# One encoder layer with PEER experts on one core: two pieces of TensorE work stand earlier, three top-k units later, and four row pairs are handled by VectorE inside the gate round

## The reference

```
proj = x @ w_in                              # 512 tokens, D = 1024
a_out = spatial_gating(...); r_out = retention(...)
h = layer_norm(ALPHA * x + concat(a_out, r_out) @ w_out)

def peer(h, w_q, sub_keys, u_tab, v_tab):    # 128*128 experts, 8 heads, 16 chosen per head
    q = (h @ w_q).reshape(b, s, 8, 2, 128)
    scores = einsum('bshpd,hpnd->bshpn', q, sub_keys)
    top_s, top_i = top_k(scores, 16)         # per half, 128 keys
    ... # 256 sums of pairs, the 16 best: expert_idx, gates = softmax
    act = gelu(einsum('td,ted->te', h, u_tab[expert_idx]))
    return einsum('te,ted->td', gates * act, v_tab[expert_idx])

x = layer_norm(ALPHA * h + peer(h))
```

## Time and profile before

| | |
|---|---|
| median of 3 runs | 1390.03 us (1389.23 to 1395.6) |
| the profiled execution | 1392.22 us, its span 1390.2 us |
| TensorE busy | 1341.3 us, 96% of the span |
| VectorE busy | 1082.9 us, 78% |
| ScalarE, GpSimd busy | 385.7 us, 697.5 us |
| granted clock, mean | 0.988 |
| TensorE starts the first act | 410.58 us |
| the gate round on TensorE | 635.82 to 706.45 us |
| DMA | 444.22 MB, mean 320 GB/s, over 410 GB/s in most slices behind the round |

### The profile page before, as it was taken

One profiled execution on the slowest core, in us unless ns is written; L12 is line 12 of the kernel. 1 busy time (PEld: TensorE's weight loads), 2 busy tenths in 40 slices (PEclk: granted clock), 3 DMA queues, 4 the chain that ended last, 5 costly groups with the idle time before them and its releaser, 6 DMA issues.

```text
span 1390.2 us, 17959 instructions
## 1 busy us (share of the span) xinstructions
PE 1341.3 (96%) x6450; PEld 947.9 (68%) x6450; DVE 1082.9 (78%) x2459; ACT 385.7 (28%) x790; POOL 697.5 (50%) x548
## 2 busy tenths in 40 slices
PE   8999998979999999999999999999999999999996
PEld 6788755568888888887754445558888885444442
DVE  4837264699999999767996779798988889666567
ACT  4213200241220102017940025656664102000000
POOL 2325111367544548751057656545754667666370
PEclk9999999989999999999999999999999999999998
DMA  7421064489999999996169999999999999999994
GB/s 250 141 79 61 2 241 130 151 295 400 381 336 382 353 367 401 413 413 273 62 237 414 414 414 413 406 366 382 381 375 375 395 413 413 414 414 414 415 414 181
DMA packets 118424, 444.22 MB, mean 320 GB/s; under 512 B 11712, under 2 KB 24512, under 8 KB 101952
## 3 DMA queue, kind: packets, MB, share of 16 engines
q0 software_dynamic: 73728, 268.47, 49.7%
q1 hardware_dynamic: 44032, 173.56, 32.2%
q10 hardware_dynamic: 576, 1.05, 0.2%
HBM read 440.94 MB, written 2.10 MB: 319 GB/s over the span
## 4 chain that ended last, share of the span: by engine, by line
PE 82%; ACT 4%; DVE 4%; DMA 3%; PEld 2%; issue 1%; ACTq 1%; DVEq 1%; PEldq 1%; POOL 0%; SPq 0%
PE ps L1469 33%; PE ps L1557 30%; PE ps L1486 7%; DMA pool_mem<-in_peer_w_q_dram 2%; PE ps L1740 2%; PEld ps L1469 2%; PE ps L1649 2%; ACT wr L700 2%; ACT wr L702 1%; PE ps L1670 1%; PE ps L1643 1%; PE ps L1541 1%; ACTq L701 1%; PE ps L1617 1%; DVE nw L886 1%
## 5 line engine op out<-in xcount | busy, mean ns | idle before, releaser
L636 POOL DMA_INDIRECT big<-in_peer_u_dram,idx x256 | 330.7, 1292 | 353.7 <-DVE dots L1248 270.1
L650 POOL DMA_INDIRECT big<-in_peer_v_dram,idx x256 | 305.9, 1195 | 164.4 <-DVE y L1273 105.9
L1273 DVE SCALAR_TENSOR_TENSOR y<-big,wgt,y 128x1024 f32<-128x1024 f32 x256 | 328.1, 1281 | 71.8 <-DMA big<-in_peer_v_dram,idx 68.3
L1248 DVE CUSTOM_DVE_ANT_0 big<-big,xh 128x1024 f32<-128x1024 f32 x256 | 310.9, 1216 | 42.6 <-DMA big<-in_peer_u_dram,idx 42.2
L1557 PE MATMUL ps<-big,pool_mem 128*128 128x512 f32 x496 | 217.4, 593 | 0.0
L1469 PE MATMUL ps<-xT,big 128*128 128x256 f32 x960 | 211.1, 380 | 0.0
L1469 PEld LDWEIGHTS ps<-xT,big 128*128 128x128 f32 x960 | 181.7, 190 | 24.3
L1557 PEld LDWEIGHTS ps<-big,pool_mem 128*128 128x128 f32 x496 | 93.7, 190 | 114.8 <-issue 114.8
L1557 PE MATMUL ps<-y,pool_mem 128*128 128x512 f32 x256 | 113.6, 594 | 0.0
L1469 PE MATMUL ps<-xT,pool_mem 128*128 128x256 f32 (+1 forms) x512 | 102.5, 360 | 5.0 <-ACTq L792 2.4
L1557 PE MATMUL ps<-xT,pool_mem 128*128 128x512 f32 x240 | 106.4, 594 | 0.0
(11 more groups left out here) (295 smaller groups left out, 1537.8 us busy)
## 6 DMA issues: line engine op xcount, KB each, us to landing
big<-u_pairs_dram SPq DMA_DIRECT2D x32, 1024.0 KB, 8.2
big<-v_pairs_dram SPq DMA_DIRECT2D x32, 1024.0 KB, 8.0
y<-u_pairs_dram SPq DMA_DIRECT2D x16, 1024.0 KB, 8.2
xT<-u_pairs_dram SPq DMA_DIRECT2D x16, 1024.0 KB, 7.9
y<-v_pairs_dram SPq DMA_DIRECT2D x16, 1024.0 KB, 8.0
xT<-v_pairs_dram SPq DMA_DIRECT2D x16, 1024.0 KB, 8.0
big<-in_w_in_dram SPq DMA_DIRECT2D x24, 512.0 KB, 5.7
pool_mem<-in_peer_w_q_dram SPq DMA_DIRECT2D x12, 1024.0 KB, 11.3
```

The source lines that it names most:

```text
L636: nc.gpsimd.indirect_dma_start(urow[n % RING], None, peer_u2, bass.IndirectOffsetOnAxis(ap=idx[:, u, e:e + 1], axis=0)).then_inc(s_u[n % R ...
L650: nc.gpsimd.indirect_dma_start(vrow[place], None, peer_v2, bass.IndirectOffsetOnAxis(ap=idx[:, u, e:e + 1], axis=0)).then_inc(s_v[place], 16)
L1248: V.tensor_tensor_reduce(out=urow[n % RING], in0=urow[n % RING], in1=xh[:, u // PH * D:(u // PH + 1) * D], scale=1.0, scalar=0.0, op0=ALU. ...
L1273: V.scalar_tensor_tensor(acc_rows[t], vrow[place], wgt[:, u % 2, e:e + 1], acc_rows[t], ALU.mult, ALU.add).then_inc(s_vadd, 1)
```

## The change

Six edits: (1) the job "outA" 1, 1 stands ahead of "hT" 0, 0 instead of behind the second "keys0". (2) The product of "query" 0 with tiles 0 and 1 is a job of its own, "queryA", one ahead of "hT" 3, 0 and one behind "hT" 3, 1; "query" 0 does the rest. (3) Units 6, 7 and 8 start at rows 79, 86 and 93 instead of 58, 71 and 84. (4) The opening and the round stand one row later. (5) Four row pairs, 106 to 109, are handled inside the round, behind groups 4, 11, 18 and 25, and left out behind it. (6) The team rows, one-hots for the gates of r = 1, stand four rows later, so that as many groups of them stand in front of the same job, and the job "gates" one act later.

```
-OPENING_ROW, ROUND_ROW = 103, 105
+OPENING_ROW, ROUND_ROW = 104, 106
+ROWS_IN_ROUND = {4: 106, 11: 107, 18: 108, 25: 109}
...
-    first = {(0, 1): ROUND_ROW + 1, (1, 0): ROUND_ROW + 28, (1, 1): ROUND_ROW + 58}[r, s]
+    first = {(0, 1): ROUND_ROW + 1, (1, 0): ROUND_ROW + 31, (1, 1): ROUND_ROW + 61}[r, s]
...
-UNIT_ROWS = {2: 9, 3: 22, 4: 35, 5: 45, 6: 58, 7: 71, 8: 84}
+UNIT_ROWS = {2: 9, 3: 22, 4: 35, 5: 45, 6: 79, 7: 86, 8: 93}
...
-    for kind, *arg in (("out", 0, 0), ("out", 0, 1), ("outA", 1, 0), ("hT", 0, 0), ("hT", 0, 1),
-                       ("query0", 0), ("keys0", 0), ("query0", 1), ("keys0", 1), ("outA", 1, 1),
+    for kind, *arg in (("out", 0, 0), ("out", 0, 1), ("outA", 1, 0), ("outA", 1, 1), ("hT", 0, 0), ("hT", 0, 1),
+                       ("query0", 0), ("keys0", 0), ("query0", 1), ("keys0", 1),
...
-                       ("hT", 1, 0), ("hT", 1, 1), ("hT", 2, 0), ("hT", 2, 1), ("dnorm", 3), ("hT", 3, 0),
-                       ("hT", 3, 1)):
+                       ("hT", 1, 0), ("hT", 1, 1), ("hT", 2, 0), ("hT", 2, 1), ("dnorm", 3),
+                       ("queryA", 0, 0), ("hT", 3, 0), ("hT", 3, 1), ("queryA", 0, 1)):
...
-            if (r, n) == (0, 19):
+            if (r, n) == (0, 20):
                 jobs.append(("gates", (), None))
...
                         if g + 1 < GROUPS:
                             first_key(g + 1)
+                        if g in ROWS_IN_ROUND:
+                            product_row(ROWS_IN_ROUND[g])
+                            add_row(ROWS_IN_ROUND[g] - LAG)
...
+                if n in ROWS_IN_ROUND.values():
+                    continue
                 if FIRST_ROWS <= n < ROWS:
                     product_row(n)
...
+                elif kind == "queryA":
+                    p = arg[1]
+                    pe.wait_ge(s_wq[TILE0 % 2], 16 * (TILE0 // 2 + 1))
+                    pe.wait_ge(s_hT, 2 * GATHERED)
+                    product(bank[:, 0:256], lambda k: wq[:, TILE0 % 2, k, p * P:(p + 1) * P],
+                            lambda k: hT[:, 0, k, :], KC)
+                    continue
```

More of the change, by code:

```diff
@@ L278, in static_jobs @@
             continue
-        if kind == "out" and arg[0] < 2:
-            b, n = next((b, n) for k, a, _, b, n in placed if k == "outA" and a == arg)
+        if kind == "out" and arg[0] < 2 or kind == "query" and arg[0] == 0:
+            b, n = next((b, n) for k, a, _, b, n in placed if k == kind + "A" and a == arg)
             placed.append((kind, arg, by, b, n))
@@ L681, in _ @@
                     continue
-                if kind in ("early", "expert"):
+                if kind in ("early", "expert", "queryA"):
                     continue
@@ L1560, in _ @@
                     continue
-                if n and not (kind == "out" and arg[0] < 2):
+                if n and not (kind == "out" and arg[0] < 2 or kind == "query" and arg[0] == 0):
                     pe.wait_ge(free[b], n)
@@ L1683, in _ @@
                     t0 = 0 if HEAD_ORDER[i_] >= TILE0 else 1
[L1684 to L1689, removed]
+                    if i_ == 0:
+                        pe.wait_ge(s_hT, 2 * NT)
+                    else:
+                        if p == 0:
+                            pe.wait_ge(s_wq[n_ % 2], 16 * (n_ // 2 + 1))
+                        product(bank[:, t0 * P:256], lambda k: wq[:, n_ % 2, k, p * P:(p + 1) * P],
+                                lambda k: hT[:, 0, k, t0 * P:], KC)
                     last = product(bank[:, 256:], lambda k: wq[:, n_ % 2, k, p * P:(p + 1) * P],
```

## The result

The changed kernel takes 1401.85 us (median of 6 runs, 1399.85 to 1404.56), the kernel before 1390.97 in 6 runs: a ratio of 1.0077 [1.0057, 1.0097]. I had forecast 1379.5. Its profiled execution took 1401.46 us, with a span of 1399.5.

The account below looks back on a forecast made before the run. TensorE's queue was taken to bound the kernel (busy 1341.3 of 1390.2 us), gathered rows close behind. From 1390.03 us, -5.7 - 9.2 + 4.2 = -10.7 gave 1379.4, stated as 1379.5; range 1375.5 to 1385.5, likeliest 1377 to 1382.5.

Parts of the forecast that it names:

- First and second gap: TensorE's idle times ahead of "hT" 0, 0 and around "hT" 3: filling them with moved jobs wins 5.7 and 9.2 us.
- Both terms by the clock: In the queries behind the two filled gaps TensorE's clock stays up: 2.3 us at the first, 2.75 at the second.
- Before the round: From queries to opening: wq loads keep their distance, VectorE arrives about 9 us before it is needed; 0 us lost.
- give-back: Part of the front's gain lost before the round through wq loads: taken as 0, between -2.3 and +4 us.
- within 3 us of selT: Sign at the opening: VectorE waits for selT or arrives at most 3 us behind it.
- the 3.8 us: At the opening: TensorE's wait for VectorE if nothing came of the moved units, with VectorE arriving at 620.
- The round: Gate round: four row pairs cost 6.3 us, ScalarE's covered waits give back 2.1, so it grows by 4.2 us.
- the 0.7 waits for ScalarE: In the round: TensorE's three waits of 0.7 us behind an early gelu are covered, winning 2.1 us.
- Behind the round: Five pairs fewer left: rows end 12 us earlier relative to TensorE, worth nothing, as TensorE needs the same 670 us.
- signs that I had named for being wrong: VectorE over 9 us behind selT at the opening, wq waits over 6 us, or a round longer by over 7.
- The rival for slower: Gates behind the four pairs: waits lower TensorE's clock, costing 20.6 us against 14.9, so 1395.7 us; chance 0.03.

Follow-up runs that it names:

- experiment 1: The changed kernel without row pairs in the round, team rows at their old distance, the moved jobs of the front kept: 1377.22 us, 0.9902.
- experiment 2: The changed kernel with SyncE loading the second layer norm's weights sooner, behind block pair 40: 1392.30 us, 1.0008.
- experiment 3: The changed kernel with ScalarE's exp and gelu of units 9 and 10 four acts earlier: 1392.49 us, 1.0014.
- experiment 4: The changed kernel with the edits of experiment 2 and experiment 3 together, pairs kept: 1383.88 us, 0.9946.
- experiment 5: The changed kernel with the edits of experiment 1, experiment 2 and experiment 3 together, so without pairs: 1377.44 us, 0.9882.
- experiment 7: The changed kernel with two row pairs in the round, behind groups 11 and 25, team rows 2 further off and not 4: 1382.90 us, 0.9947.
- experiment 8: The changed kernel with the team rows four row pairs sooner in VectorE's order, pairs kept: 1385.30 us, 0.9948.
- experiment 9: The kernel of experiment 1 with units 6, 7 and 8 back at rows 58, 71 and 84: 1380.03 us, 0.9908.
- experiment 10: The kernel of experiment 1 run again on the same chip as experiment 9: 1379.03 us, 0.9906.
- experiment 11: The kernel of experiment 1 with "half" 0 and 1 ahead of the last act and unit 5's gelu two acts sooner: 1375.08 us, 0.9891.
- experiment 12: The edit of experiment 11 with two row pairs as in experiment 7 and the edits of experiment 2 and experiment 3: 1376.31 us, 0.9903.
- experiment 6: The kernel before with only the four row pairs in the round and team rows four rows later: 1414.26 us, 1.0155.

## Why the prediction was wrong, step by step

**First and second gap: right.** The forecast was 5.7 + 9.2 = 14.9; the head start is 15.4 in the queries and 14.1 at the acts and at the round, of which 0.8 isn't the change's. One execution gives it only roughly: in the profiles of all kernels with this front (the changed one and experiments 1 to 5 and 7 to 12) the round begins between 620.56 and 624.18 us, 11.6 to 15.3 us ahead of the kernel before. Both terms by the clock came too: 1.00 where the earlier trace rows have 0.50. The windows of TensorE at the two places of the earlier trace rows:

```profile
216.00:220.00 4.00, 3.94 (x35) 1.00 0.00 0
287.00:291.00 4.00, 4.00 (x20) 1.00 0.94 330
```

**Before the round: nearly right.** I took 0 for give-back, and 1.3 us were lost between the queries and the acts. TensorE waits for wq as long as before (2.4 us, now in one wait), but behind that wait 32 records take 7.03 us where the same ones took 5.48. VectorE comes to the opening at 609.0 us (forecast 607.5) and later waits 7.89 us for TensorE's first gate (7.90 in the earlier trace rows):

```profile
609.02 0.29 DVE L1323 CAST pieces<-work 128x256 f16<-128x256 f32 x1
...
625.50 0.69 DVE L1335 SCALAR_TENSOR_TENSOR pool_mem<-ps,pool_mem 128x512 f32<-128x512 f32 x1 [7.89 <-PE ps L1741]
```

That VectorE arrives within 3 us of selT was the forecast. That the moved units bring it there sooner holds too (experiment 9, by 10.8 us); the 3.8 us that this was to save were 1.2.

**The round: right in size (4.3 for 4.2), and that in part by luck.** Four waits of 1.49 to 1.67 us, where I had about 1.55, and the 0.7 waits for ScalarE have gone. But the clock fell where I had said it wouldn't, three times: at the start of the round, and behind the waits for the pairs of groups 11 and 18. TensorE's windows at the first two places:

```profile
627.00:629.20 2.20, 2.20 (x14) 0.50 1.01 411
...
653.00:655.50 2.50, 2.50 (x19) 0.56 0.84 290
```

Four early records take 2.04 us there (627.41 in the timeline above); in the round of the kernel before they take 1.09, so each such stretch costs about 1 us, 3 in all. Against that the groups in which ScalarE was ahead ran in 1.90 us and not 2.06, 0.15 us less in each of some 22. Neither term was in the forecast, and they happen to cancel.

**Behind the round: this is the step that failed.** I had written that the lead of the rows "is worth nothing at the end: TensorE needs the same 670 us from the round to its last product", and "team rows and 'gates' keep their distance or come earlier". The first is true only of the end. TensorE needed 689.5 us. I gave the lead of the rows no price on the way. The lead of 16 us ran into two places where nobody had waited before, with margins of 0.1 and 3.1 us, and the team one-hots behind them were late: 15 us of waiting and 4 of slow clock. Experiments 2, 3 and 4 take the waits away one by one (9.5, 9.4 and 18.0 us), 6 makes them in the kernel before, and 7 halves the lead. The second sentence was wrong too. I counted the distance of the team rows in rows; four of those rows had been done in the round, so that for VectorE the distance was the same as before; but with the rows ahead the same distance no longer stops them: at their two buffers the team's one-hots hold VectorE for 7.97 us, and four rows sooner for 25.3 (experiment 8). The edit let the lead through. None of the signs that I had named for being wrong came (VectorE late at the opening, over 6 us of waits for wq, a round longer by over 7): all of them lie before the end of the round.

With the two waits mended the kernel with pairs takes 1383.9 us, 4.4 above my number and inside the range. Its profiled span is 8.0 us below that of the kernel before, which is -12.2 at the start of the round and +4.2 in it: the forecast's other terms hold there, and what is missing lies in the front and in the scatter of its start. Apart from that the pairs cost the round 4.2 us and bring nothing: without them the rows end 2.5 us before they are needed (1.1 to 2.6 in the profiles of 1, 5 and 9 to 11), so there was nothing to be won by taking pairs from behind the round. The prediction says so in its own first paragraph, and should have drawn from it that the change is best without its pairs. The front alone takes 1377.22 us and, run again, 1379.03. (Between experiments 4 and 1 the ratios differ by 6.1 us; 4.2 of them are the round, and in the profiled executions the round of 4 begins 3.0 us later than that of 1 but only 0.8 later than that of 10, the same kernel again, so this is the scatter.)

**The rival for slower** named the wrong place. Its price stood on the clock behind waits in the round, its threshold on a wait of over 2.5 us. The clock did fall behind shorter ones, and cost about 1 us a time, and the kernel got slower for another reason. The Trainium skill ("TensorE: Matmul & The Clock Gate", HAM oscillation) tells of a kernel that waits for a DMA in each pass of a loop and is throttled anew by each of these waits. By that rule the waits in the round and behind it have a second price beside their length. The trace agrees in part: the granted clock is 0.50 to 0.58 behind five of them (the first one, those of groups 11 and 18, A and B) and 1.00 behind those of groups 4 and 25.

## What to carry to other kernels

An engine that works off a fixed order and is made earlier pays at the first wait whose releaser didn't come earlier with it. So list, for the engine that gains time, each wait that now shows nothing, with the time from its release to its use (here 0.1 and 3.1 us), and ask who paces the releaser and who waits for what is queued behind. The time to spare at the end says nothing of this.

A lead can be spent where nobody minds: at a buffer which the other engine empties, just ahead of its need. Before such a distance is made longer, look what it holds back. And of two such waits each mended alone shows half; only both together, and both without the change, tell that the loss is understood.

## What the runs showed of the hardware

The granted clock fell behind waits shorter than I had thought. Behind one of 1.52 us in the round it was 0.56 for 2.5 us, behind one of 1.49 it was 0.50 from 671.0 to 673.7. Behind those of 1.66 and 1.67 us, of the same kind in the same round, it stayed at 1.00 (636 to 639 and 684 to 690). Behind the 2.47 us wait at the start of the round it was 0.50 in the changed kernel. In the kernel before, the same wait of 2.47 us ends at 638.94, and TensorE's window behind it has full clock:

```profile
640.00:644.00 4.00, 4.00 (x41) 1.00 1.00 409
```

The length of a wait alone doesn't decide. What does is open.

TensorE's three waits of 0.7 us for ScalarE behind an early gelu stayed when "half" had a lead of two groups (experiment 11), and went when VectorE held TensorE back by 1.5 us. Why the lead wasn't enough is open too.
